# Order of work around the first and the last expert item of a hybrid decoder block: index product, mixing weights, last but one item's rows, final gain

## The reference

```python
h = x
h = h + hybrid_mixer(rms_norm(h, norm_mix_g), ...)      # gated DeltaNet + short convolution
h = h + moe_ffn(rms_norm(h, norm_ffn_g), ...)           # top 4 of 32 experts
return rms_norm(h, norm_final_g)
```

```python
logits = xf @ w_router + b_router
top_vals, top_idx = lax.top_k(logits, 4);  top_w = softmax(top_vals)
# for each block of at most 128 tokens of one expert e:
gu = xb @ w_gate_up[e] + b_gate_up[e]
gate = minimum(gu[:, :1024], 7.0);  up = clip(gu[:, 1024:], -7.0, 7.0)
hid = (up + 1.0) * gate * sigmoid(1.702 * gate)
y = hid @ w_down[e] + b_down[e]
out[token] += y * weight_of_choice
```

## Time and profile before

| what | value |
| --- | --- |
| median of three runs | 1824.86 us |
| the profiled execution, its own time | 1825.08 us |
| its span between first and last instruction | 1823.3 us |
| TensorE busy | 1789.1 us (98%) |
| VectorE busy | 1452.3 us (80%) |
| ACT busy | 1100.8 us (60%) |
| POOL busy | 714.2 us (39%) |
| mean DMA rate over the span | 276 GB/s |

### The profile page before, as it was taken

How to read it: one execution, slowest core, us unless ns; L and a number is a source line. 1 busy time by engine, 2 the same in 40 slices (tenths; PEclk the granted TensorE clock), 3 DMA queues, 4 the chain that set the end, 5 groups by cost and what they waited for, 6 DMA issues and landing times.

```text
span 1823.3 us, 23880 instructions
## 1 busy us (share of the span) xinstructions
PE 1789.1 (98%) x8584; PEld 1492.8 (82%) x8584; DVE 1452.3 (80%) x1073; ACT 1100.8 (60%) x900; POOL 714.2 (39%) x392
## 2 busy tenths in 40 slices
PE   8999999999999998999999999999999999999996
PEld 6888888897888887888888888888888888888885
DVE  4336667674334689999999999999999999999996
ACT  4223563343332356777777777777777777777774
POOL 1000112420000015654664565466456446646644
PEclk9999999999999999999999999999999999999999
DMA  5223424004442658999999999999999999999995
GB/s 186 94 93 107 171 73 137 18 9 183 149 129 93 231 202 321 379 372 389 375 376 378 377 379 373 385 377 369 380 379 377 373 385 372 378 380 377 377 369 184
DMA packets 126912, 503.90 MB, mean 276 GB/s; under 512 B 25192, under 2 KB 25400, under 8 KB 93780
## 3 DMA queue, kind: packets, MB, share of 16 engines
q1 hardware_dynamic: 114400, 478.57, 68.4%
q0 software_dynamic: 10128, 24.40, 5.7%
q10 hardware_dynamic: 2340, 0.33, 0.1%
HBM read 485.66 MB, written 26.26 MB: 281 GB/s over the span
## 4 chain that ended last, share of the span: by engine, by line
PE 92%; DVE 4%; ACT 2%; DMA 1%; issue 1%; POOL 0%; POOLq 0%; SPq 0%; DVEq 0%; ACTq 0%
PE PB L2375 12%; PE PB L2376 12%; PE PB L2378 12%; PE PB L2282 11%; PE PB L2395 6%; PE PB L2392 6%; PE PB L2393 6%; PE PB L1967 4%; PE PB L1968 4%; PE PB L1969 4%; PE PB L2100 2%; PE PB L2347 2%; PE PB L2355 2%; PE PB L2341 1%; PE PB L2247 1%; DVE acc L1439 1%
## 5 line engine op out<-in xcount | busy, mean ns | idle before, releaser
L523 DVE TENSOR_TENSOR mlo<-mraw,mhi 128x2048 fp32r<-128x2048 f32 x384 | 908.2, 2403 | 51.4 <-ACT mhi L519 51.3
L519 ACT ACTIVATE mhi<-mraw 128x2048 fp32r<-128x2048 f32 x384 | 718.7, 1913 | 107.5 <-PE PB L2378 103.6
L2375 PE MATMUL PB<-mhi,xgT_hi 128*128 128x512 f32 x1012 | 397.4, 393 | 2.7 <-DVE mlo L523 1.6
L2376 PE MATMUL PB<-mlo,xgT_hi 128*128 128x512 f32 x1012 | 394.5, 390 | 0.0
L2378 PE MATMUL PB<-mhi,xgT_lo 128*128 128x512 f32 x1012 | 270.7, 389 | 0.0
L893 POOL TENSOR_TENSOR glu<-glu 128x1024 f32<-128x1024 f32 x32 | 80.9, 2527 | 455.4 <-DVE glu L1853 455.4
L2375 PEld LDWEIGHTS PB<-mhi,xgT_hi 128*128 128x128 f32 x1012 | 190.0, 188 | 43.1 <-DVE mlo L523 2.4
L2378 PEld LDWEIGHTS PB<-mhi,xgT_lo 128*128 128x128 f32 x1012 | 189.9, 188 | 39.9
L2376 PEld LDWEIGHTS PB<-mlo,xgT_hi 128*128 128x128 f32 x1012 | 190.1, 188 | 38.9
L2392 PE MATMUL PB<-mhi,hT_hi 128*128 128x512 f32 x496 | 195.9, 395 | 0.0
L2393 PE MATMUL PB<-mlo,hT_hi 128*128 128x512 f32 x496 | 193.2, 389 | 0.0
(11 more groups left out here) (371 smaller groups left out, 2764.5 us busy)
## 6 DMA issues: line engine op xcount, KB each, us to landing
mraw<-in_w_gate_up_dram SPq DMA_DIRECT2D x256, 1024.0 KB, 9.3
mraw<-in_w_down_dram SPq DMA_DIRECT2D x128, 1024.0 KB, 7.1
raw<-in_w_in_dram SPq DMA_DIRECT2D x27, 1024.0 KB, 4.9
qkvT<-in_w_in_dram SPq DMA_DIRECT2D x8, 1024.0 KB, 4.9
qkvT<-in_w_o_gdn_dram SPq DMA_DIRECT2D x4, 1024.0 KB, 5.0
qkvT<-in_w_o_sconv_dram SPq DMA_DIRECT2D x4, 1024.0 KB, 5.0
qkvT<-in_w_mix_out_dram SPq DMA_DIRECT2D x4, 1024.0 KB, 4.9
qkvT<-in_x_dram SPq DMA_DIRECT2D x4, 512.0 KB, 5.1
```

What stands on the lines that cost most here:

```text
L519: nc.scalar.activation(mhi[split_slot(m)][:], mraw[:, raw_slot(m), :], ACT.Copy).then_inc(e_h, 1)
L523: nc.vector.tensor_tensor(mlo[split_slot(m)][:], mraw[:, raw_slot(m), :], mhi[split_slot(m)][:].bitcast(F32), ALU.subtract).then_inc(e_l, 1)
L2375: pe.matmul(gate_up_bank[:, n, :], xgT_hi[:, k, :], w_hi[:, n, :], start=False, stop=False)
L2376: pe.matmul(gate_up_bank[:, n, :], xgT_hi[:, k, :], w_lo[:, n, :], start=False, stop=False)
```

## The change

Six edits, on all engines:

1. `index_products` moves on TensorE from behind chunk k = 4 to before its last four matmuls; on VectorE the split of chunk 9 moves from ahead of the index's three steps to behind them.
2. The four operations on the mixing weights move on POOL from ahead of the gather for item 2 to behind the first `slot_weights`, and wait for the split of item 0's chunk 4; ACT's two copies of them move from ahead of the loop to behind it.
3. On TensorE the down product of the last but one item holds only the mixing turn, behind its third chunk; the hidden turn and the first bias product come behind it.
4. ACT does the last but one item's y rows, with a semaphore of their own, ahead of the hi part of the last hidden rows; VectorE does the last item's chunk 2 ahead of their lo part. Both parts are made in two halves, and `last_down` waits for each half where it needs it.
5. `scatter` is cut in two functions, `aim` (copies of row numbers) and `add_rows`; for the last but one item `step` comes ahead of the wait for the y rows.
6. SP loads the final gain row when `mix_w` is ready and the last weights are issued, not behind the last scatter.

```diff
@@ -523,8 +523,9 @@
...
+        HALVES = (slice(0, GT), slice(GT, KD))
...
-        INDEX_AFTER = 4
+        INDEX_WITHIN = 4
...
@@ -730,8 +732,9 @@
...
+    sp.wait_ge(s_mixw, TOPK)
+    sp.dma_start(final_gain[:], norm_final_g.partition_broadcast(P)).then_inc(s_fg, 16)
     sp.wait_ge(s_stored, 1)
-    sp.dma_start(final_gain[:], norm_final_g.partition_broadcast(P)).then_inc(s_fg, 16)
     for t in range(TT):
...
@@ -892,14 +895,14 @@
...
-    def scatter(i):
+    def aim(i):
         nc.gpsimd.tensor_copy(now[:, 1:2], index[:, bass.ds(i, 1)]).then_inc(s_goal, 1)
         pool.wait_ge(s_ws, 16 * i + 16)
         nc.gpsimd.tensor_copy(now[:, 2:3], target[:, bass.ds(i + 1, 1)]).then_inc(s_wrow, 1)
         pool.wait_ge(s_goal, i + 1)
         pool.wait_ge(s_wrow, i + 2)
-        pool.wait_ge(s_y, i + 2)
-        step()
+
+    def add_rows(i):
         nc.gpsimd.indirect_dma_start(sum_d, bass.IndirectOffsetOnAxis(ap=now[:, 1:2], axis=0), y_rows[:], None,
...
@@ -918,6 +921,17 @@
...
                         weight[:].rearrange("p (t k) -> p t k", t=TT)).then_inc(s_wout, 16)
+    pool.wait_ge(s_tx, 1)
+    gather(2)
+    hidden(0)
...
+    nc.gpsimd.tensor_copy(now[:, 2:3], target[:, 0:1]).then_inc(s_wrow, 1)
+    pool.wait_ge(s_wrow, 1)
+    pool.wait_ge(s_wout, 16)
+    step(2)
+    slot_weights()
...
+    pool.wait_ge(e_l, chunk_number(0, 4) + 1)
     nc.gpsimd.tensor_tensor(mixing[:], chosen[:], weight[:].unsqueeze(2).to_broadcast([P, K4, E]),
...
@@ -926,16 +940,7 @@
...
         nc.gpsimd.tensor_tensor(mix_w[:], mix_w[:], by_choice[:, :, k, :], ALU.add).then_inc(s_mixw, 1)
-    pool.wait_ge(s_tx, 1)
-    gather(2)
-    hidden(0)
...
-    nc.gpsimd.tensor_copy(now[:, 2:3], target[:, 0:1]).then_inc(s_wrow, 1)
     nc.gpsimd.tensor_copy(goal_f[:, 0:1], index[:, bass.ds(last, 1)]).then_inc(s_goalf, 1)
-    pool.wait_ge(s_wrow, 1)
-    pool.wait_ge(s_wout, 16)
-    step(2)
-    slot_weights()
...
@@ -945,10 +950,16 @@
...
-        scatter(i)
+        aim(i)
+        pool.wait_ge(s_y, i + 2)
+        step()
+        add_rows(i)
     pool.wait_ge(s_th, last)
     hidden(last)
-    scatter(last - 1)
+    aim(last - 1)
+    step()
+    pool.wait_ge(s_before_last, 1)
+    add_rows(last - 1)
     pool.sem_inc(s_stored, 1)
...
@@ -1282,17 +1293,22 @@
...
-    def hidden_hi(i, to=hT_hi):
+    def hidden_hi(i):
         act.wait_ge(s_th, i + 1)
-        nc.scalar.activation(to[:], turn_bank, ACT.Copy).then_inc(s_hh, 1)
...
-    def y_copy(i):
+        nc.scalar.activation(hT_hi[:], turn_bank, ACT.Copy).then_inc(s_hh, 1)
...
+    def last_hidden_hi():
+        act.wait_ge(s_th, last + 1)
+        for ks in HALVES:
+            nc.scalar.activation(xgT_hi[:, ks, :], turn_bank[:, ks, :], ACT.Copy).then_inc(s_hh, 1)
...
+    def y_copy(i, done=s_y):
...
-                             scale=slot_weight).then_inc(s_y, 1)
+                             scale=slot_weight).then_inc(done, 1)
...
@@ -1304,9 +1320,6 @@
...
     sigmoid(0)
-    act.wait_ge(s_mixw, TOPK)
-    for n in range(2):
-        nc.scalar.activation(mix3[:, :, n * E:(n + 1) * E], mix_w[:], ACT.Copy).then_inc(s_mix3, 1)
...
@@ -1325,14 +1338,17 @@
...
+    act.wait_ge(s_mixw, TOPK)
+    for n in range(2):
+        nc.scalar.activation(mix3[:, :, n * E:(n + 1) * E], mix_w[:], ACT.Copy).then_inc(s_mix3, 1)
     products_hi(last - 1)
     weights_hi(act, last - 1, 12)
+    weights_hi(act, last - 1, 13)
     act.wait_ge(s_mixT, 1)
     nc.scalar.activation(mix_wT[:], PM[0:3 * E, 3, :].rearrange("p (t s) -> p t s", t=TT), ACT.Copy).then_inc(s_mixc, 1)
-    weights_hi(act, last - 1, 13)
-    hidden_hi(last, xgT_hi)
     weights_hi(act, last, 2)
-    y_copy(last - 1)
+    y_copy(last - 1, s_before_last)
+    last_hidden_hi()
     weights_hi(act, last, 3)
...
@@ -1823,13 +1839,13 @@
...
-    weights_lo(dve, -1, 9)
     dve.wait_ge(s_idx, 1)
...
     nc.vector.tensor_scalar(index[:, 0:ITEMS], target[:], 2, None, ALU.logical_shift_right).then_inc(s_index, 1)
+    weights_lo(dve, -1, 9)
     weights_lo(dve, -1, 10)
...
@@ -1853,9 +1869,15 @@
...
-    def hidden_lo(i, to=hT_lo, high=hT_hi):
+    def hidden_lo(i):
         dve.wait_ge(s_hh, i + 1)
-        nc.vector.tensor_tensor(to[:], turn_bank, high[:].bitcast(F32), ALU.subtract).then_inc(s_hl, 1)
+        nc.vector.tensor_tensor(hT_lo[:], turn_bank, hT_hi[:].bitcast(F32), ALU.subtract).then_inc(s_hl, 1)
...
+    def last_hidden_lo():
+        for n, ks in enumerate(HALVES):
+            dve.wait_ge(s_hh, last + 1 + n)
+            nc.vector.tensor_tensor(xgT_lo[:, ks, :], turn_bank[:, ks, :], xgT_hi[:, ks, :].bitcast(F32),
+                                    ALU.subtract).then_inc(s_hl, 1)
...
@@ -1889,8 +1911,8 @@
...
     for m in range(11, 14):
         weights_lo(dve, last - 1, m)
-    hidden_lo(last, xgT_lo, xgT_hi)
     weights_lo(dve, last, 2)
+    last_hidden_lo()
     weights_lo(dve, last, 3)
...
@@ -2374,14 +2396,14 @@
                 for n in range(4):
                     pe.matmul(gate_up_bank[:, n, :], xgT_hi[:, k, :], w_hi[:, n, :], start=False, stop=False)
                     pe.matmul(gate_up_bank[:, n, :], xgT_hi[:, k, :], w_lo[:, n, :], start=False, stop=False)
+                if first and k == INDEX_WITHIN:
+                    index_products()
                 for n in range(4):
                     mm = pe.matmul(gate_up_bank[:, n, :], xgT_lo[:, k, :], w_hi[:, n, :], start=False,
                                    stop=(k == KD - 1))
             mm.then_inc(e_used, 1)
             if m0 == 0 and k == TURN_HIDDEN_AFTER:
                 turn_hidden(i - 1)
-            if first and k == INDEX_AFTER:
-                index_products()
...
@@ -2404,8 +2426,9 @@
...
     def last_down(after):
-        pe.wait_ge(s_hl, last + 1)
         for d in range(4):
+            if d % 2 == 0:
+                pe.wait_ge(s_hl, last + 1 + d // 2)
             down_chunk(last, d, d, last_bank, xgT_hi, xgT_lo)
...
@@ -2453,11 +2476,13 @@
...
     def second_bias():
-        pe.wait_ge(s_y, last + 1)
+        pe.wait_ge(s_before_last, 1)
         bias_product(1)
...
     gate_up(last, 0)
-    down(last - 1, {0: turn_mixing, 1: lambda: bias_product(0), 2: lambda: turn_hidden(last)})
+    down(last - 1, {2: turn_mixing})
+    turn_hidden(last)
+    bias_product(0)
     last_down({1: second_bias, 2: lambda: bias_product(2)})
...
```

More of the change, by code:

```diff
@@ L537, in hybrid_block @@
         s_th, s_hh, s_hl = sem("s_hidden_turned"), sem("s_hidden_hi"), sem("s_hidden_lo")
+        s_before_last = sem("s_y_rows_of_last_but_one")
         s_y, s_yst, s_goal = sem("s_y_rows"), sem("s_y_stored"), sem("s_target_copied")
@@ L2362, in gate_up @@
                             w_hi, w_lo = (w[split_slot(m)][:].rearrange("p (n c) -> p n c", n=4) for w in (mhi, mlo))
-                            if first and k > INDEX_AFTER:
+                            if first and k > INDEX_WITHIN:
                                 pe.wait_ge(e_h, chunk_number(i - 1, m) + 1)
```

## The result

The changed kernel takes 1827.67 us (median of 20 runs, 1826.10 to 1827.98) against 1824.94 us for the kernel before, measured beside it (20 runs, 1824.28 to 1826.79): a ratio of 1.0013, with a 95% interval of 1.0007 to 1.0019. The whole interval lies under 1.002, so the kernel is not slower by over 0.2%, but it is slower: by 2.7 us in the medians and by 2.3 in the means. The median is above the predicted range, and the forecast of 1824.4 was 3.3 us too low.

What follows compares the result with a forecast made beforehand. The prediction took TensorE to bound the kernel, with only seam and tail able to move. A seam gain of 0.9 us and a tail loss of 0.5 summed to -0.4, from 1824.86 to 1824.4 us; range 1822.4 to 1826.9.

Steps and rivals of the forecast that it cites:

- What bounds it: Whole kernel: TensorE, busy 1789.1 of 1823.3 us; only its waits, at seam and tail, or what follows it can give time.
- The seam, -0.9: Between router and experts: the tokens' low part starts at 687.7 instead of 688.62, a gain of 0.9 us.
- The clamps: VectorE at the seam: the clamps start at 685.4, after index, splits and sums, and end at 687.7.
- The mixing operations: POOL in the loop's first pass: at most 3.1 us of VectorE's time, covered by TensorE's work, costed at nothing.
- ACT's two copies: Mixing copies (0.45 us) moved behind the loop: costed at nothing, with +0.45 as the other end.
- It is ready 1.7 us sooner and starts 1.6 us later: TensorE at the last item's down product: ready near 1790.3, but starts at 1794.55 instead of 1792.97, awaiting the low part.
- The transfers: Tail: the scatter starts 1.15 us sooner, first rows are back by 1808.0, so the first add waits for TensorE.
- From there to the first put-back products the work is the same: Last item's down product: unchanged in length, so its first put-back products end at 1809.6.
- The rival: TensorE's clock falls before the last item: +1.4 to +2.7 us if short, 1836.6 us if long; chance 0.14.
- The point of decision near 3.9 us: TensorE's clock: idle stretch that decides its fall, read at the program's end; the forecast's own wait was just beyond it.
- The four adds stay back to back and the rest is unchanged: End of the kernel: adds still take 5.03 us, nothing behind them changes; the tail's loss stays 0.5 us.

Runs made afterwards that it cites:

- a_seam: Kernel before with only the index-product and mixing-operation edits (1 and 2), tail unchanged: 1823.87 us, ratio 0.9993.
- i_index: Kernel before with edit 1 alone (index products sooner, chunk 9's split behind the index): 1824.60 us, ratio 0.9998.
- j_mixing: Kernel before with edit 2 alone (mixing operations behind the first slot weights, ACT's copies behind the loop): 1824.83 us, ratio 1.0001.
- g_before_swap: Kernel before with one VectorE swap, the last item's low hidden rows behind its chunk 2 low weights: 1829.31 us, ratio 1.0024.
- b_tail: The changed kernel without edits 1 and 2, so the tail's edits alone on the kernel before: 1827.99 us, ratio 1.0018.
- e_order_warm: Changed kernel with VectorE's last low hidden rows ahead of chunk 2's split again, plus 8 overwritten products before the last bias product: 1822.87 us, ratio 0.9989.
- c_warm2: Changed kernel with 17 overwritten 512-column products on TensorE ahead of the last item's bias product, profiled once: 1825.35 us.

## Why the prediction was wrong, point by point

- **What bounds it:** right. Both stretches were the ones that moved, and nothing in the loop changed for the time.
- **The seam, -0.9:** right, -0.94 in the profile and -1.0 in a_seam, and for the reason given: the traces of i_index and j_mixing show VectorE's string and the gather each holding the low part when only the other is shortened. The clamps started at 685.69 (685.4 plus 0.27 of the stretch ahead). The mixing operations cost nothing in the loop's first pass, and ACT's two copies nothing either.
- **"It is ready 1.7 us sooner and starts 1.6 us later":** right. The start came 1.64 us later against the item before, the wait was 4.35 us of the 4.0 to 4.4 forecast.
- **The transfers:** right. The scatter was issued 1.86 us sooner, 1.16 of it from the tail and 0.70 from ahead of it, and the first add waits for TensorE. That it also landed sooner after its issue (6.3 instead of 8.1 us) moved nothing, since it was hidden.
- **"From there to the first put-back products the work is the same":** this is the step that failed. The work is the same, the clock is not. The product took 14.60 us instead of 12.33. The rival had it, with the right size (+1.4 to +2.7; it was +2.27), and a chance of 0.14. The wait that I had worked out myself, 4.0 to 4.4 us, was longer than the only idle stretch from which I took a point of decision (3.9 us), so by its own rule the fall was the likelier case, and the forecast should have been 1824.4 + 2.3 = 1826.7.
- **The point of decision near 3.9 us:** wrong as well. Here the clock fell at 1791.9, 2.4 us after the end of the last matmul, in g_before_swap at 1794.1, 2.4 us after 1791.72, but in b_tail only 4.7 us after it, when matmuls ran again. At the program's end, where the prediction had read its 3.9 us, it fell 2.1 us after the last matmul in e_order_warm and 4.8 us after it in the changed kernel. One stretch at the program's end was one sample, not a threshold.
- **"The four adds stay back to back and the rest is unchanged":** the second step that failed, +0.84 less 0.19. The finish of VectorE and POOL's addition were 0.02 us apart in the trace before. Nothing in the text looked behind the adds, and no rival had it. With the clock's term alone the sum is 1826.7, inside the range, which ended at 1826.9; with this one too it is 1827.35, outside and 0.3 under the measured median.

The Trainium skill ("SBUF — State Buffer", section "Who interferes with whom") was used in the prediction for the seam and spoke there of two engines that lock each other out for a whole instruction. The rows of the final norm agree with it: a 128x1 operation of 0.22 us takes 1.26 beside a finish of about 1.2 us. The prediction did not apply it there.

## What to carry to other kernels

An order on a helper engine is not free because that engine is off the path: ask how long it leaves TensorE idle in one piece, since the price of a longer piece can be the wait and, on top, half the clock over 3 to 6 us of the work behind it (shown here behind waits of 3.7 and 4.35 us, inferred for 2.1). If such a wait can't be removed, products whose result is overwritten keep the clock, at no cost while they fit in the wait. When the end of a string shifts by even tenths of a microsecond, read what stands behind it: two engines that just miss each other before may meet after. And where two strings meet, measure edits in pairs, since each alone shows nothing.

## What the runs showed of the hardware that was not expected

**At the seam** of the changed kernel the granted clock was 0.61 and 0.54 in the two stretches from 689 to 693 us, and the eight hi and lo products of the second item's first chunk ran 0.43 us apart. No single wait there is longer than 0.70 us, but TensorE is idle in pieces for about 1.5 of the 3 us before.

The changed kernel by stretches, columns as in the earlier trace rows:

```profile
689.00:691.00 2.00, 1.70 (x4) 1.39 (x5) 2.00 (x3) 2.00 (x2) 0.61 (x1) 0.61 0.99 315
691.00:693.00 2.00, 2.00 (x6) 1.54 (x5) 2.00 (x2) 2.00 (x2) 2.00 (x1) 0.54 0.89 367
```

In i_index the same stretches had 0.56 and 0.58; in a_seam and c_warm2, with the same order as the changed kernel, the clock was 1.00. It cost nothing: VectorE is busy throughout both stretches and sets the pace, and TensorE waits for its split behind them in any case (0.33 us).

**Two groups.** The changed kernel's 20 runs lie in two groups too, six of 1826.1 to 1826.5 us and fourteen of 1827.2 to 1828.0. The mean granted clock is 0.997 in the first and 0.995 or 0.996 in the second, so a part of it is probably the clock, but which stretch differs was not seen: the one profile is of the second group. The profile of b_tail shows two things that could make the first: a fall that lasts 3.4 us instead of 6.8 (0.66 us on the product) and a last addition of POOL that meets no finish (0.3 us). Together they are 0.9 of the about 1.3 us between the groups. That they are what happened in the changed kernel is not shown.
